# Two neighbouring rows of the down weight on one partition, and every second gate and up column to match

## The reference, cut to what matters

```
# per expert e; x_rows: the tokens that chose e; D = 1024, FE = 3584
hidden = silu(x_rows @ w1[e]) * (x_rows @ w3[e])     # (rows, 3584)
y      = hidden @ w2[e]                              # (rows, 1024)
# y is weighted by the gate of each token and added to the residual
```

## Time and profile before

| | |
|---|---|
| median of three runs | 2270.48 us (2266.92 to 2270.74) |
| the profiled execution's own time | 2261.01 us |
| its span, first to last instruction | 2259.3 us |
| mean granted TensorE clock | 0.954 of full speed |
| TensorE busy (matmul) | 2029.3 us, 90% |
| TensorE weight loads busy | 1794.6 us, 79% |
| VectorE, ScalarE, GpSimd busy | 70%, 49%, 4% |
| DMA | 457 MB, mean 202 GB/s |
| loads of expert weights | 336 of 1024 KB |

### The profile page before, as it was taken

How to read it: one execution, slowest core, us unless ns; L and a number is a source line. 1 busy time by engine, 2 the same in 40 slices (tenths; PEclk the granted TensorE clock), 3 DMA queues, 4 the chain that set the end, 5 groups by cost and what they waited for, 6 DMA issues and landing times.

```text
span 2259.3 us, 32314 instructions
## 1 busy us (share of the span) xinstructions
PE 2029.3 (90%) x12128; PEld 1794.6 (79%) x12129; DVE 1572.0 (70%) x1628; ACT 1096.8 (49%) x924; POOL 94.3 (4%) x101
## 2 busy tenths in 40 slices
PE   7899999999999882999899898898999998998993
PEld 6778788888787772999899776677998778998772
DVE  6765534543575844788688788787888687888786
ACT  5532432333354232555555566566555566555663
POOL 0000000000000003000100100100000001000001
PEclk9999999999999995999999999999999999999996
DMA  5312623323222015677676799898776898776994
GB/s 193 98 57 66 224 74 111 96 83 100 93 75 75 29 42 149 235 250 258 224 258 234 258 328 331 299 329 303 260 253 232 296 333 307 252 257 237 318 321 157
DMA packets 214901, 457.31 MB, mean 202 GB/s; under 512 B 7649, under 2 KB 58865, under 8 KB 214849
## 3 DMA queue, kind: packets, MB, share of 16 engines
q1 hardware_dynamic: 204880, 420.50, 54.4%
q0 software_dynamic: 9968, 36.05, 4.4%
HBM read 436.60 MB, written 19.94 MB: 202 GB/s over the span
## 4 chain that ended last, share of the span: by engine, by line
PE 56%; DVE 15%; DMA 11%; issue 9%; ACT 8%; POOL 1%; DVEq 0%; SPq 0%; ACTq 0%; POOLq 0%
PE ps L915 11%; PE ps L559 10%; PE ps L560 10%; PE ps L561 10%; DMA raw<-in_moe_w_dram 9%; DVE w_lo L1798 6%; PE ps L932 6%; PE ps L917 5%; ACT w_hi L1169 4%; PE ps L934 2%; DVE w_lo L1325 1%; ACT w_hi L1012 1%; DMA raw<-in_w_in_dram 1%; PE ps L620 1%; DVE scores L1442 1%
## 5 line engine op out<-in xcount | busy, mean ns | idle before, releaser
L1798 DVE TENSOR_TENSOR w_lo<-raw,w_hi 128x2048 fp32r<-128x2048 f32 x340 | 775.6, 2288 | 219.7 <-ACT w_hi L1169 210.5
L1169 ACT ACTIVATE w_hi<-raw 128x2048 fp32r<-128x2048 f32 x340 | 645.6, 1912 | 298.9 <-DMA raw<-in_moe_w_dram 234.7
L915 PE MATMUL ps<-xt,w_hi 128*128 128x320 f32 x1792 | 472.0, 350 | 9.9 <-issue 9.9
L917 PE MATMUL ps<-xt,w_lo 128*128 128x160 f32 x1792 | 426.7, 238 | 0.0
L915 PEld LDWEIGHTS ps<-xt,w_hi 128*128 128x128 f32 x1792 | 339.5, 189 | 10.7 <-issue 10.6
L917 PEld LDWEIGHTS ps<-xt,w_lo 128*128 128x128 f32 x1792 | 345.3, 193 | 0.1
L559 PE MATMUL ps<-act_hi,w_hi 128*128 128x512 f32 x608 | 240.7, 396 | 14.4 <-DVE act_lo L1363 7.2
L932 PE MATMUL ps<-ht,w_hi 128*128 128x320 f32 x896 | 234.8, 347 | 6.6 <-DVE fold L1835 6.6
L560 PE MATMUL ps<-act_lo,w_hi 128*128 128x512 f32 x608 | 238.6, 393 | 0.0
L561 PE MATMUL ps<-act_hi,w_lo 128*128 128x512 f32 x608 | 238.6, 392 | 0.0
L934 PE MATMUL ps<-ht,w_lo 128*128 128x160 f32 x896 | 212.4, 237 | 0.0
(11 more groups left out here) (313 smaller groups left out, 3026.7 us busy)
## 6 DMA issues: line engine op xcount, KB each, us to landing
raw<-in_moe_w_dram SPq DMA_DIRECT2D x336, 1024.0 KB
raw<-in_w_in_dram SPq DMA_DIRECT2D x20, 1024.0 KB
raw<-in_ffn_w_gate_dram SPq DMA_DIRECT2D x11, 1024.0 KB
raw<-in_ffn_w_up_dram SPq DMA_DIRECT2D x11, 1024.0 KB
raw<-in_ffn_w_down_dram SPq DMA_DIRECT2D x11, 1024.0 KB
raw<-in_w_out_dram SPq DMA_DIRECT2D x8, 1024.0 KB
y_rows<-yacc POOLq DMA_DIRECT2D x8, 1024.0 KB, 6.2
y_rows<-mult POOLq DMA_DIRECT2D x1, 7168.0 KB, 21.4
```

Source lines behind the costliest of these rows:

```text
L915: pe.matmul(pairs_of(ps[:, bank, 0:2 * NW]), hi_[:, k % 4, f * P:(f + 1) * P], xt[:, k, :, 0:NW], start=k == 0, stop=False)
L917: last = pe.matmul(ps[:, bank, NW:2 * NW], lo_[:, k % 4, f * P:(f + 1) * P], xt[:, k, 0, 0:NW], start=False, stop=k == KT - 1)
L1169: act.activation(slot_hi[p % 6], raw[:, n % 3, :], ACT.Copy).then_inc(w_hi_done, 1)
L1798: dve.tensor_tensor(slot_lo[p % 6], raw[:, n % 3, :], f32(slot_hi[p % 6]), ALU.subtract) \
```

## The change

Three places, all in the expert part. Down pieces are loaded with `"x (p k) n -> p (x k) n"`: rows 2p and 2p + 1 of the 256 lie on partition p. They are neighbours in memory and in SBUF, so each partition gets one run of 8 KB. Half k of a piece now holds the rows of parity k. To match, block f of the hidden columns is no longer columns 128f to 128f + 127 but, by the new function `columns`, the even (f % 2 = 0) or odd (f % 2 = 1) columns of the 256 that belong to down piece f // 2. `turn` takes these columns of `hid_e` as stationary operand, and `turned_up` takes these columns of `w_hi` and `w_lo`: 128 elements at a step of 2 elements (8 bytes). The number of matmuls, weight loads, loads of pieces, waits and increments is the same.

```
-                            .rearrange("x (k p) n -> p (x k) n", p=P)
+                            .rearrange("x (p k) n -> p (x k) n", p=P)
...
+            def columns(f):
+
+                return slice(f // 2 * GW + f % 2, (f // 2 + 1) * GW, 2)
+
...
             def turn(b, q, step):
...
-                    last = pe.transpose(ps[:, 4, f * P:(f + 1) * P], hid_e[:, b, f * P:(f + 1) * P], idt[:, :])
+                    last = pe.transpose(ps[:, 4, f * P:(f + 1) * P], hid_e[:, b, columns(f)], idt[:, :])
...
             def turned_up(kind, f, p, c_at):
...
-                    pe.matmul(pairs_of(ps[:, bank, 0:2 * NW]), hi_[:, k % 4, f * P:(f + 1) * P],
+                    pe.matmul(pairs_of(ps[:, bank, 0:2 * NW]), hi_[:, k % 4, columns(f)],
                               xt[:, k, :, 0:NW], start=k == 0, stop=False)
-                    last = pe.matmul(ps[:, bank, NW:2 * NW], lo_[:, k % 4, f * P:(f + 1) * P],
+                    last = pe.matmul(ps[:, bank, NW:2 * NW], lo_[:, k % 4, columns(f)],
                                      xt[:, k, 0, 0:NW], start=False, stop=k == KT - 1)
```

## The result

The changed kernel has a median of 2276.72 us over 13 runs (2269.39 to 2285.40) against 2267.62 us over 13 runs of the kernel before (2265.31 to 2271.75). The ratio is 1.0041, with a 95% interval of 1.0027 to 1.0055: 9 us slower, beyond what a measurement can tell from no change. The forecast was 2267.3 us with a range of 2261 to 2277. The median lies just inside the upper end of the range, but on the other side of before.

What follows compares the result with a forecast made beforehand. TensorE was taken to bound the turned items, DMA engines at 0.90 to 0.93 the others. Loads -3.2 us, weight loads 0, transposes 0: 2270.5 - 3.2 = 2267.3 us, range 2261 to 2277.

Steps and rivals of the forecast that it cites:

- I take 0, for this reason from rows: Gate and up weight loads in turned items: stepped columns add 0, needing no more SBUF bytes per ns than a stream.
- The working around it: Turned items, 1792 pairs: second weight load of each pair open, first covered by 23 ns or so; pair every 0.26 us.
- X: Extra ns of a stepped weight load in the turned items, costing at least 1792 X.
- Its own sign of being wrong: Turned items: pairs should still start every 0.26 us; at 0.27 or more the forecast is wrong.
- The rival: Stepped weight loads at L915 and L917 in turned items are slower, up to 358 us if doubled; chance 0.17.
- The price of a doubled load, 358 us: Turned items: if stepped loads double, a pair goes from 0.26 to 0.46, 1792 x 0.2 = 358 us.
- the transposes' 12 us: The 112 transposes of `turn` with stepped columns: 12 us at most at twice 0.11 us, nothing expected.
- Packets: Down-piece loads: 128 packets of 8 KB instead of 256 of 4 KB, 0.309 to 0.310 us each.
- I pass on 0.9 of it: Items waiting for loads: of 3.6 us saved over 56 down pieces, 3.2 us shorten the kernel, DMA engines busy 0.90.
- the forecast's 0.9986: Ratio expected for 8 KB loads without stepped columns if they give what was forecast, about 3 us less.
- The chain in the earlier trace: One raw slot in a load-waiting item: load 5.30 us, rounding 1.92, subtraction 2.31; 3.22 us a piece, 135 of 147 us.
- the prediction's 5 to 17 ns per packet: Expert loads: 5 to 6 ns per packet while streaming, 17 ns saved per merge with starts of pieces included.

Runs made afterwards that it cites:

- the loads alone: Down pieces loaded in runs of 8 KB, neighbouring columns kept everywhere, against the kernel before (output not the reference's): ratio 1.0004 (0.9990 to 1.0017).
- the halves: ScalarE's rounding and VectorE's subtraction of each expert piece in two halves, loads and columns unchanged, against the kernel before: 2258.36 us, ratio 0.9961.

## Why the prediction was wrong

- **Weight loads, the step that failed.** "I take 0, for this reason from rows": the stepped load asks for 9.3 bytes per ns, no more than the streamed operand gets. The extra is 7 to 8 ns on a load of 110. That a stream gets 9.6 bytes per ns of neighbours says nothing of a weight load, which no row had shown above 4.7 (512 bytes in 110 ns). The working around it was right: X above 2 ns takes back the gain, above 4.3 ns the kernel is slower beyond noise; one load of the pair is open and the other covered; 1792 pairs. With X = 7.5 it gives 13.4 us, and the turned items lost 13.5, though the medians moved by 9 only. Its own sign of being wrong, a pair at 0.27, came (0.268). The rival had the sign and the place and was given 0.17; a bound with 0 at one end and 358 us at the other, and a break-even at 2% of the load's time, wanted more.
- The price of a doubled load, 358 us, was measured as 362 at a step of 16 bytes; the transposes' 12 us, for loads twice as long, aren't in it, and their loads didn't double.
- **Packets.** 0.309 us for 8 KB as forecast, 128 of them instead of 256.
- **"I pass on 0.9 of it", the other step that failed.** About 0 of it passed: the loads alone are at 1.0004, and the forecast's 0.9986 lies outside their interval. A DMA share of 0.90 was read as nine tenths bound by transfers. The chain in the earlier trace rows pointed at what bounds: a slot's loop, 9.67 us for three pieces, with the rounding and the subtraction in it. That the slot of the chain held only gate and up pieces could have been counted from the code.
- The transposes: their four starts of 0.11 us became 0.12, about 1 us in 112. The sentence of the Trainium skill that crossings to a new line are paid for, in "SBUF — State Buffer", section "Door 1: The DMA port swizzle (why `[64,N]` ≈ `[32,N]`)", was the one that held: the loads got longer at two hits a line (198 ns shown instead of 189 and 193), so its other sentence, that two hits hide the access, doesn't hold for weight loads here. VectorE's read at the same step shows no such cost (2288 against 2287 ns), and the transposes' loads, longer at 8 bytes, didn't get longer again at 16 (207 and 209 ns), where there is one hit a line.

Not settled: why the medians moved by 9 us where the turned items lost 13.5, and what 8 KB runs give where transfers alone are the bound. No kernel here was in that state beyond doubt, and each comparison with and without them lies within its interval.

## What to carry to other kernels

Before pricing an edit on a transfer, follow the chain once round: a buffer ring's pace is load plus processing of the slowest slot, a high DMA share doesn't prove that transfers bound it, and with pieces of several kinds count which kind falls in which slot. Where stationary operands are reloaded behind short streams, a weight load that gets longer is paid in full; keep their columns next to each other, and if data must be interleaved, do it where the engine's time is free (here VectorE's instruction got no longer and ScalarE's did; with VectorE alone it wasn't tried). When a break-even is a few ns times a count in the thousands, an argument for zero needs a row that shows the operation itself.

## What the runs showed of the hardware

- A weight load of 128 columns of w_hi or w_lo, four bytes each, at a step of 8 bytes takes some 7% longer (about 8 ns), at 16 bytes about twice as long (0.23 against 0.11 us). The transposes' weight loads, of float32, start every 0.12 us instead of 0.11 at 8 bytes and are shown as long at 16 (209 against 207 ns).
- In the trace of the halves TensorE waits 3.5 us until 1596.7 us, and its granted clock is 0.51 from 1595 to 1602 us. In the items for up to 128 tokens the mean clock differs between executions (0.95 and 0.92), and their lengths with it (147 and 151 us).
- ScalarE's copy of 2048 elements from SBUF takes 2.09 us at a read step of 8 bytes, in blocks of 128, instead of 1.91; VectorE's two-operand subtraction doesn't change (2.29 us).
- Cutting a row's work in two costs VectorE 2 x 1.22 us for 2.29, and ScalarE 2 x 1.05 for 1.91.
- With down pieces in 512 packets instead of 256 the kernel took 13 us more, 0.23 us for each of the 56 pieces, at a mean clock of 0.950 instead of 0.953. By the prediction's 5 to 17 ns per packet, 16 more on each engine, it would be 0.08 to 0.27 us of an engine. In the other direction nothing passes on.
